# First feed-forward product by seven products instead of eight (Strassen), in a one-core encoder layer in float32

## Chip, cores and metric

One core of one Trainium2 chip runs the kernel. The metric is the device time of one execution in microseconds (us). Five engines work side by side: TensorE (PE; its weight loads are listed as PEld), VectorE (DVE), ScalarE (ACT), GpSimd (POOL) and SyncE (SP), whose queue starts the DMAs. They meet only at semaphores; each engine takes its own instructions in the order in which the program lists them.

## The reference, cut to what matters

The program is one layer of an encoder for 1024 prompt tokens and 128 sample tokens: an input projection, three mixers (forgetting attention, pooling, attention to a memory), a gated merge, an output projection, and a feed-forward part. The change is about the last two lines, and a little about the column block `f` of the input projection.

```
z = rmsnorm(x, g_attn) @ w_in          # ... f: 8 forget logits, logf = log_sigmoid(f + b_f)
h = x + m @ w_out                      # m: the gated sum of the three mixers
a = relu(rmsnorm(h, g_mlp) @ w_up)     # w_up 1024 x 4096
y = h + (a * a) @ w_down               # w_down 4096 x 1024
```

All is float32. The 1152 tokens of both groups go through the weights together.

## The kernel before

**Products in two parts.** A float32 operand is split into a high part that TensorE takes in its `fp32r` form (a rounding copy by ACT, `activation(..., Copy)`) and a low part (DVE: operand minus high part). A product is three matmuls, `COMBOS`: high by high, high by low, low by high. A weight tile is 128 rows by 128 columns for each of the 8 slices of the model width (`KT` = 8), a block is one output tile by a third of the tokens (`TB` = 384 columns), so a block over the model width is 8 x 3 = 24 matmuls of 384 columns. Blocks go to three PSUM banks in turn (`bank(b)`, banks 5 to 7); `emptied(eng, b)` waits until the block has been read out, `finished(eng, b)` until its matmuls are done.

**Order.** There is no scheduler: `plan` is a list of steps (`add(kind, i, j, ...)`), and each engine's program walks through it and issues its own share of every step (`for s in plan[FIRST:]`), with extra work hung beside a step by `put(...)`. For the steps `out`, `up`, `down` and `last`:

- `out` n (8 of them, 3 blocks of 24 matmuls): one tile of `m @ w_out`. DVE adds the block to `H`, ACT and DVE write the next product's operand `A` (times `g_mlp`, high and low) and the squares for the norm.
- `up` (8 rounds of 4 tiles, 3 blocks each): one row tile of `w_up`. DVE reads the block (`ff_r`: relu times 1/rms, L2041), squares it (`ff_a`, L2044) and subtracts the high part that ACT made of it (`ff_hi` L1497, `ff_lo` L2047).
- `down` (7 rounds of 8 tiles, 3 blocks of 12 matmuls): the four tiles of `up` times `w_down`, added to `H` by DVE (L2052). `last` is the eighth round, with its weights (`w_last`) loaded as a whole, and the output norm beside it.

Weights of all these steps come by one DMA a tile, are split by `split_hi` (ACT, L444) and `split_lo` (DVE, L451), and are kept twice (`W[c % 2]`), so a tile is made ready while the one before it is used.

**The start.** `early` makes the first blocks beside the normalisation of x. The forget logits are 8 columns, but the tile loaded for them is 128 columns wide, and takes the same 24 matmuls a block as any other.

**GpSimd** makes constants at the start and sixteen small copies for the sample tokens (L800), and nothing from 802 us on.

## Time and profile before

| | |
|---|---|
| median of 3 runs | 2033.2 us (2032.01 to 2034.89) |
| the profiled execution | 2032.71 us; its span 2031.0 us |
| PE busy | 1969.2 us (97%), 11755 matmuls; granted clock 0.994 |
| DVE busy | 992.2 us (49%) |
| ACT busy | 690.5 us (34%) |
| POOL busy | 10.7 us (1%) |
| DMA | 164.7 MB, mean 81 GB/s |
| PE in 1212.2 to 1964.3 us (`up` and `down`) | busy all of 752.1 us |

The span runs from the first to the last instruction; the time is 1.7 us longer. A busy share adds up instruction durations, and matmuls overlap: a matmul of 384 columns is listed with about 0.33 us, while one starts every 0.174 us. So PE's pace is read from distances between starts, or from a count over a stretch, not from durations.

### The profile page before, as it was taken

To read this page: it belongs to the slowest core of one execution; us is meant where nothing else is said; L and a number is where in the kernel's file an instruction comes from. 1 tells how busy PE (TensorE), PEld (TensorE's weight loads), DVE (VectorE), ACT (ScalarE), POOL (GpSimd) and SP (SyncE) were. 2 spreads that over 40 slices of the span, in tenths; PEclk is the share of its full clock that TensorE was granted. 3 is DMA by queue.
4 is the path that set the end of the run, shared out by engine and by line. 5 is a ranking of instruction groups with operands and counts; after the bars stand their busy time and mean duration, and the time that the engine had idled before them with its cause. 6 is when DMAs were issued, how large, how long until landed. Compare 5 with 4: busy or idle time off the path is not lost.

```text
span 2031.0 us, 28635 instructions
## 1 busy us (share of the span) xinstructions
PE 1969.2 (97%) x11755; PEld 1936.3 (95%) x11755; DVE 992.2 (49%) x1895; ACT 690.5 (34%) x1299; POOL 10.7 (1%) x45
## 2 busy tenths in 40 slices
PE   7998999999989999999999999999999999999998
PEld 7998899999989989999999999999999999999998
DVE  6674545454446656554433455444343434344434
ACT  6444546364555545443222332111111111111112
POOL 0000000000000000000000000000000000000000
PEclk9999999999999999999999999999999999999999
DMA  6442221212245544254223311020202020202202
GB/s 189 111 111 61 57 84 37 82 56 69 72 155 179 167 149 130 89 165 149 82 79 91 89 54 42 27 58 27 58 27 57 27 57 27 57 27 57 69 26 93
DMA packets 208087, 164.72 MB, mean 81 GB/s; under 512 B 14287, under 2 KB 186319, under 8 KB 207446
## 3 DMA queue, kind: packets, MB, share of 16 engines
q1 hardware_dynamic: 207957, 162.90, 26.4%
q8 instruction: 93, 1.52, 0.3%
q14 instruction: 37, 0.30, 0.0%
HBM read 133.36 MB, written 29.51 MB: 80 GB/s over the span
## 4 chain that ended last, share of the span: by engine, by line
PE 81%; issue 6%; ACT 6%; DVE 5%; DMA 2%; SPq 0%; ACTq 0%; DVEq 0%
PE ps L1150 68%; PE ps L1134 2%; PE ps L986 2%; PE ps L976 1%; PE ps L822 1%; ACT fox_p L1299 1%; PE ps L909 1%; ACT fox_pt_hi L1306 1%; PE ps L943 1%; ACT fox_p L1311 1%; ACT w_hi L444 1%; PE ps L919 1%; DVE fox_pt_lo L1729 1%; DMA foxs_kraw<-in_cache_fox_k_dram 0%; PE ps L1056 0%
## 5 line engine op out<-in xcount | busy, mean ns | idle before, releaser
L1150 PE MATMUL ps<-act_hi,w_hi 128*128 128x384 f32 x1800 | 612.7, 340 | 4.7 <-DVE fox_v L1995 3.5
L1150 PE MATMUL ps<-act_hi,w_lo 128*128 128x384 f32 x1800 | 603.2, 335 | 0.0
L1150 PE MATMUL ps<-act_lo,w_hi 128*128 128x384 f32 x1800 | 602.9, 335 | 0.0
L1150 PEld LDWEIGHTS ps<-act_hi,w_hi 128*128 128x128 f32 x1800 | 338.7, 188 | 6.6 <-issue 5.7
L1150 PEld LDWEIGHTS ps<-act_lo,w_hi 128*128 128x128 f32 x1800 | 338.9, 188 | 0.7
L1150 PEld LDWEIGHTS ps<-act_hi,w_lo 128*128 128x128 f32 x1800 | 338.3, 188 | 0.0
L444 ACT ACTIVATE w_hi<-w_raw 128x1024 fp32r<-128x1024 f32 (+1 forms) x173 | 148.1, 856 | 302.4 <-PE ps L1150 300.8
L451 DVE TENSOR_TENSOR w_lo<-w_raw,w_hi 128x1024 fp32r<-128x1024 f32 (+1 forms) x173 | 168.8, 976 | 133.2 <-ACT w_hi L444 133.2
L1150 PE MATMUL ps<-ff_hi,w_hi 128*128 128x384 f32 x672 | 227.1, 338 | 0.0
L1150 PE MATMUL ps<-ff_lo,w_hi 128*128 128x384 f32 x672 | 227.1, 338 | 0.0
L1150 PE MATMUL ps<-ff_hi,w_lo 128*128 128x384 f32 x672 | 227.1, 338 | 0.0
L2052 DVE TENSOR_TENSOR h<-ps,h 128x384 f32<-128x384 f32 x192 | 106.9, 557 | 222.5 <-PE ps L1150 199.1
L1497 ACT ACTIVATE ff_hi<-ff_r 128x384 fp32r<-128x384 f32 x96 | 50.4, 525 | 325.7 <-DVE ff_r L2041 325.7
L2041 DVE SCALAR_TENSOR_TENSOR ff_r<-ps,rstd 128x384 f32<-128x384 f32 x96 | 53.4, 557 | 185.1 <-PE ps L1150 185.1
L1150 PEld LDWEIGHTS ps<-ff_hi,w_hi 128*128 128x128 f32 x672 | 126.2, 188 | 0.0
L1150 PEld LDWEIGHTS ps<-ff_hi,w_lo 128*128 128x128 f32 x672 | 126.2, 188 | 0.0
L1150 PEld LDWEIGHTS ps<-ff_lo,w_hi 128*128 128x128 f32 x672 | 126.2, 188 | 0.0
L1150 PE MATMUL ps<-branch_hi,w_hi 128*128 128x384 f32 x288 | 102.0, 354 | 0.0
L1150 PE MATMUL ps<-branch_hi,w_lo 128*128 128x384 f32 x288 | 98.2, 341 | 0.0
L1150 PE MATMUL ps<-branch_lo,w_hi 128*128 128x384 f32 x288 | 98.1, 341 | 0.0
L1729 DVE TENSOR_TENSOR fox_pt_lo<-ps,fox_pt_hi 128x128 fp32r<-128x128 f32 (+3 forms) x64 | 48.5, 758 | 86.2 <-ACT fox_pt_hi L1306 85.9
L1573 ACT ACTIVATE gate<-ps 128x384 f32<-128x384 f32 x72 | 35.3, 490 | 103.2 <-PE ps L1150 103.2
(306 smaller groups left out, 2830.3 us busy)
## 6 DMA issues: line engine op xcount, KB each, us to landing
w_raw<-in_w_in_dram SPq DMA_DIRECT2D x45, 512.0 KB, 4.5
w_raw<-in_w_up_dram SPq DMA_DIRECT2D x32, 512.0 KB, 4.1
w_raw<-in_w_down_dram SPq DMA_DIRECT2D x56, 256.0 KB, 2.8
merged<-prod SPq DMA_DIRECT2D x48, 192.0 KB, 1.9
prev<-merged SPq DMA_DIRECT2D x48, 192.0 KB, 4.2
foxs_kraw<-in_cache_fox_k_dram SPq DMA_DIRECT2D x8, 1024.0 KB, 5.2
foxs_vraw<-in_cache_fox_v_dram SPq DMA_DIRECT2D x8, 1024.0 KB, 5.7
out_dram<-fin_y SPq DMA_DIRECT2D x9, 512.0 KB, 2.6
```

The source lines that it names most:

```text
L444: nc.scalar.activation(W[c % 2][0][:, 0:kt, :], w_raw[c % 2][:, 0:kt, :], ACT.Copy).then_inc(w_hi[c % 2], 1)
L451: nc.vector.tensor_tensor(W[c % 2][1][:, 0:kt, :], w_raw[c % 2][:, 0:kt, :], W[c % 2][0][:, 0:kt, :].bitcast(F32), ALU.subtract).then_inc( ...
L822: last = nc.tensor.matmul(bank(s.b)[:, 0:TB], W[k][a][:, t, :], A[z][:, t, cols(s.j)], start=(t == 0 and n == 0), stop=(t == KT - 1 and n ...
L909: last = nc.tensor.matmul(ps[:, 4, lo:2 * P], fv[:, x, 2 * h:2 * h + 2, :], fpt[z][:, x, lo:2 * P], start=(x == 0 and z == 0), stop=(x == ...
L986: last = nc.tensor.matmul(ps[:, 4, :], b["pt"][x][:, t, :], b["v"][y][:, t, :], start=(n == 0 and t == 0), stop=end)
L1134: last = nc.tensor.matmul(bank(s.b)[:, 0:TB], LW[a][:, t, s.j * P:(s.j + 1) * P], AC[(NCH - 1) % 2][z][:, t, cols(s.i)], start=(t == 0 and ...
L1150: last = nc.tensor.matmul(bank(b)[:, 0:width], W[k][a][:, t, :], moving[z][:, t, j * width:(j + 1) * width], start=(t == 0 and n == 0), st ...
L1497: nc.scalar.activation(AC[s.i % 2][0][:, s.j, cols(j)], ff_r[i % 2][:], ACT.Square).then_inc(ff["hi"], 1)
L1573: nc.scalar.activation(gate[:, cols(j)], src, ACT.Tanh, scale=0.5).then_inc(free, 1)
L1729: nc.vector.tensor_tensor(dst[1][:, 0:blocks, cs], turned_tiles()[:, 0:blocks, :], dst[0][:, 0:blocks, cs].bitcast(F32), ALU.subtract).the ...
L2041: nc.vector.scalar_tensor_tensor(out=ff_r[i % 2][:], in0=src, scalar=0.0, in1=rstd[:, cols(j)], op0=ALU.max, op1=ALU.mult).then_inc(free, 1)
L2052: nc.vector.tensor_tensor(h, src, h, ALU.add).then_inc(free, 1)
```

## The change

**Strassen on `up`.** The product of `w_up` with h is taken in pairs of row tiles. With the model width cut into two halves of 4 slices (`HK`), the weights of a pair are a 2 x 2 matrix of blocks; the tokens are cut into two halves (`HALF` = 576), each half into two quarters (`TQ` = 288 columns), so that the h operand of a half is 2 x 2 as well. Seven products (m = 0 to 6) of sums of such blocks take the place of eight: 7 x 4 x 3 = 84 matmuls of 288 columns for a pair of row tiles and a half of the tokens. There are 16 pairs x 2 halves = 32 such groups g, two to each step `up(c)`, and they come as `up(0) up(1) down(0) up(2) down(1)` and so on; `down(c)` takes place for one half of the tokens. Around the seven products stands new work:

- the h operands: 7 sums for each slice (`BS`, `BO`), on ACT, DVE and POOL, once for each half of the tokens;
- the weight operands: for each group five sums of 128x512 on POOL (`weight_sum`), seven rounding copies on ACT (`weight_hi`) and seven subtractions on DVE (`weight_lo`). Each of the seven operands has one buffer (`WO[m]`), so product m of a group must be over before that of the next group is made;
- the results: ACT copies five of the seven products out of PSUM (c3, c4, c1, c5, c2 in that order), POOL makes two combined terms of them by four instructions of 128x288 (`copies_sum`), DVE adds one of the four terms to a product still in PSUM (`result`, first instruction), multiplies by 1/rms (second), and squares and splits (`square_lo`, two more). PSUM banks 0 to 4 take the products in turn; a bank is free for the product five later only once it has been read.

**`out`, `down`, `last`** go by quarters of the tokens: 4 blocks of 288 columns where there were 3 of 384. A `down` step holds two output tiles (weights 128x1024 at once).

**Forget logits.** Only the 8 columns are loaded; their high parts go to columns 0 to 7 and their low parts to columns 32 to 39 of one tile, zeroed by POOL, so two matmuls a slice do (`pairs`) where there were three; DVE adds the two halves of the result.

**Smaller**: several semaphores are merged, DVE makes `g_neg` behind the load of `g_mlp`, the 1/rms is made once for each half of the tokens.

The core of the diff:

```diff
+    HALF, TQ = T // 2, T // 4
+    HK = KT // 2
+    PAIRS_UP = FT
...
+    for c in range(2 * NCH):
+        up(c)
+        if c % NCH:
+            down(c - 1)
+        if c == NCH - 1:
+            down(c)
...
+            def weight_sum(g, m):
...
+                if g:
+                    pool.wait_ge(up_s["over"], 7 * (g - 1) + m + 1)
...
+                nc.gpsimd.tensor_tensor(WS[m][:], up_raw(g, *a), up_raw(g, *b), op).then_inc(uw["sum"], 1)
...
+            def copies_sum(g, n):
+                pool.wait_ge(up_s["copied"], 5 * g + 4 + n)
+                a, out = ((c4, c5), (c3, c2))[n]
+                nc.gpsimd.tensor_tensor(out[:], a[:], out[:], ALU.subtract).then_inc(up_s["e"], 1)
+                pool.wait_ge(up_s["e"], 4 * g + 2 * n + 1)
+                nc.gpsimd.tensor_tensor(out[:], out[:], c1[:], ALU.add).then_inc(up_s["e"], 1)
...
+            def up_product(g, x):
...
+                pe.wait_ge(uw["lo"], 7 * g + x + 1)
+                if 7 * g + x >= 5:
+                    bank_left(pe, *divmod(7 * g + x - 5, 7))
...
+                        last = nc.tensor.matmul(up_bank(g, x), WO[x][a][:, t, :], BO[x][z][:, t, :],
+                                                start=(t == 0 and n == 0), stop=(t == HK - 1 and n == 2))
...
+                    nc.scalar.activation((c3, c4, c1, c5, c2)[x][:], up_bank(g, x), ACT.Copy).then_inc(up_s["copied"], 1)
...
+            def weight_lo(g, m):
+                dve.wait_ge(uw["hi"], 7 * g + m + 1)
...
+                nc.vector.tensor_tensor(WO[m][1][:], src, WO[m][0][:].bitcast(F32), ALU.subtract).then_inc(uw["lo"], 1)
...
+            def result(g, n, other):
...
+                nc.vector.tensor_tensor(out[:], up_bank(g, x), other[:], ALU.add).then_inc(up_s["step"], 1)
...
+                nc.vector.scalar_tensor_tensor(out=out[:], in0=out[:], scalar=0.0,
+                                               in1=rstd[:, quarter(2 * g // PAIRS_UP, RESULT[n][1])], op0=ALU.max,
+                                               op1=ALU.mult).then_inc(up_s["r"], 1)
+
+            def square_lo(i):
+                out = ff_r[i % 3]
+                dve.wait_ge(ff["hi"], i + 1)
+                nc.vector.tensor_tensor(out[:], out[:], out[:], ALU.mult).then_inc(ff["a"], 1)
+                dve.wait_ge(ff["a"], i + 1)
+                nc.vector.tensor_tensor(ff_part(1, i), out[:], ff_part(0, i).bitcast(F32), ALU.subtract).then_inc(ff["lo"], 1)
...
+                pairs = COMBOS if s.kind == "u" else ((0, 0), (0, 1))
```

The second group of an `up` step gets its weight operands 0 to 3 during the first group (`weights_at`), and 4 to 6 at its own first products; the first group of the next step gets all seven during the `down` step between.

What DVE has in its program inside `up` in the kernel before, three blocks and a weight tile (`ff_r`, `ff_a`, `ff1_lo`: the result, its square, the square's low part; `w0_lo`: the weight tile's low part; `ffn_hi` is counted up by ACT, `blk_over` by PE):

```order
L2041 SCALAR_TENSOR_TENSOR ff_r0_205<-ps,rstd_204 128x384 [waits blk_over]
L2044 TENSOR_TENSOR ff_a0_207<-ff_r0_205 128x384 [waits bank_free2]
L2047 TENSOR_TENSOR ff1_lo_203<-ff_a0_207,ff1_hi_202 128x384 [waits ffn_hi,ffn_a]
L2041 SCALAR_TENSOR_TENSOR ff_r1_206<-ps,rstd_204 128x384 [waits blk_over]
L2044 TENSOR_TENSOR ff_a1_208<-ff_r1_206 128x384 [waits bank_free0]
L2047 TENSOR_TENSOR ff1_lo_203<-ff_a1_208,ff1_hi_202 128x384 [waits ffn_hi,ffn_a]
L451 TENSOR_TENSOR w0_lo_57<-w_raw0_54,w0_hi_56 128x1024 [waits w_hi0]
```

Each result needs three instructions, of which the first reads PSUM, and each weight tile adds one more to every nine.

What DVE has in the changed kernel at the passage from the first group of an `up` step to its second (`u_c2`, `u_c5`: the terms that POOL has made, `up_e` counts POOL's steps; `ffm_lo`: low part of the squares; `u_op4_lo` to `u_op6_lo`: low parts of the second group's weight operands, `up_w_hi` is counted by ACT):

```order
L2239 TENSOR_TENSOR ff_r0_253<-ps,u_c2_252 128x288 [waits up_over,up_e]
L2243 SCALAR_TENSOR_TENSOR ff_r0_253<-ff_r0_253,rstd_197 128x288 [waits up_step]
L2239 TENSOR_TENSOR ff_r1_254<-ps,u_c5_251 128x288 [waits up_over]
L2243 SCALAR_TENSOR_TENSOR ff_r1_254<-ff_r1_254,rstd_197 128x288 [waits up_step]
L2250 TENSOR_TENSOR ff_r0_253<-ff_r0_253 128x288 [waits ffn_hi]
L2252 TENSOR_TENSOR ffm_lo_247<-ff_r0_253,ffm_hi_246 128x288 [waits ffn_a]
L2250 TENSOR_TENSOR ff_r1_254<-ff_r1_254 128x288 [waits ffn_hi]
L2252 TENSOR_TENSOR ffm_lo_247<-ff_r1_254,ffm_hi_246 128x288 [waits ffn_a]
L2232 TENSOR_TENSOR u_op4_lo_234<-u_sum4_243,u_op4_hi_233 128x512 [waits up_w_hi]
L2232 TENSOR_TENSOR u_op5_lo_236<-u_sum5_244,u_op5_hi_235 128x512 [waits up_w_hi]
L2232 TENSOR_TENSOR u_op6_lo_238<-u_sum6_245,u_op6_hi_237 128x512 [waits up_w_hi]
L2239 TENSOR_TENSOR ff_r2_255<-ps,u_c3_248 128x288 [waits up_over,up_copied]
```

Results now take four instructions, two of the group's four results stand behind POOL's `up_e`, and the weight operands that PE needs for products 4 to 6 of the second group stand behind all of the first group's results.

What POOL has in the same stretch (`u_sum`: sums of weight blocks, `u_raw1`: the loaded pair; `up_over` is counted by PE for each product, `up_copied` by ACT for each copy); before, POOL had no instruction here at all:

```order
L950 TENSOR_TENSOR u_sum2_241<-u_raw1_224 128x512 [waits up_over,u_in1]
L956 TENSOR_TENSOR u_c5_251<-u_c4_249,u_c5_251 128x288 [waits up_copied]
L958 TENSOR_TENSOR u_c5_251<-u_c5_251,u_c1_250 128x288 [waits up_e]
L950 TENSOR_TENSOR u_sum3_242<-u_raw1_224 128x512 [waits up_over]
L956 TENSOR_TENSOR u_c2_252<-u_c3_248,u_c2_252 128x288 [waits up_copied]
L958 TENSOR_TENSOR u_c2_252<-u_c2_252,u_c1_250 128x288 [waits up_e]
L950 TENSOR_TENSOR u_sum4_243<-u_raw1_224 128x512 [waits up_over]
L950 TENSOR_TENSOR u_sum5_244<-u_raw1_224 128x512 [waits up_over]
L950 TENSOR_TENSOR u_sum6_245<-u_raw1_224 128x512 [waits up_over]
```

The sum for weight operand 3 stands between the two combined terms, and the sums for operands 4 to 6 behind them.

## Rows read from the trace of the kernel before

**Rows 1.** Busy time by stretch: start:end, length, busy us (count) by engine, clock.

```profile
1212.20:1964.30 752.10, 752.10 (x4310) 752.10 (x4309) 337.97 (x548) 119.51 (x189) 0.00 (x0) 1.00 0.15 43
...
1300.00:1500.00 200.00, 200.00 (x1147) 200.00 (x1146) 85.94 (x142) 29.91 (x48) 0.00 (x0) 1.00 0.15 43
```

**Rows 2.** Chain that ended last: start us, length us, what, count of matmuls.

```profile
1212.22 752.15 PE ps L1150 x4308
```

**Rows 3.** Waits over the whole span: us in total, times, longest us.

```profile
ACT ff_hi L1497 <- DVE ff_r L2041: 325.7, 96, 6.9
...
DVE h L2052 <- PE ps L1150: 199.1, 152, 1.6
...
DVE ff_r L2041 <- PE ps L1150: 185.1, 92, 2.4
```

**Rows 4.** Timeline of PE, weights by memory tokens: start us, us, instruction; 22 between.

```profile
103.17 0.28 PE L1150 MATMUL ps<-memn_hi,w_hi 128*128 128x256 f32 x1
...
105.92 0.28 PE L1150 MATMUL ps<-memn_hi,w_lo 128*128 128x256 f32 x1
```

**Rows 5.** Instruction groups of DVE, 1205 to 1400 us: busy us, mean ns.

```profile
L2047 DVE TENSOR_TENSOR ff_lo<-ff_a,ff_hi 128x384 fp32r<-128x384 f32 x33 | 18.4, 558 | 2.3
...
L2052 DVE TENSOR_TENSOR h<-ps,h 128x384 f32<-128x384 f32 x24 | 13.4, 557 | 28.7 <-PE ps L1150 28.7
...
L451 DVE TENSOR_TENSOR w_lo<-w_raw,w_hi 128x1024 fp32r<-128x1024 f32 x11 | 13.5, 1225 | 4.0 <-ACT w_hi L444 4.0
...
L451 DVE TENSOR_TENSOR w_lo<-w_raw,w_hi 128x512 fp32r<-128x512 f32 x9 | 6.2, 690 | 1.0 <-ACT w_hi L444 1.0
...
L1914 DVE RECIPROCAL rstd<-rstd 128x384 f32<-128x384 f32 x3 | 7.4, 2514 | 1.4 <-ACT rstd L1436 1.4
```

**Rows 6.** Instruction groups of ACT in the same stretch.

```profile
L1497 ACT ACTIVATE ff_hi<-ff_r 128x384 fp32r<-128x384 f32 x33 | 17.3, 525 | 109.3 <-DVE ff_r L2041 109.3
...
L444 ACT ACTIVATE w_hi<-w_raw 128x512 fp32r<-128x512 f32 x9 | 5.6, 627 | 33.3 <-PE ps L1150 33.3
```

**Rows 7.** Timeline of DVE in `up`: start us, us, instruction.

```profile
1226.84 0.56 DVE L2041 SCALAR_TENSOR_TENSOR ff_r<-ps,rstd 128x384 f32<-128x384 f32 x1
...
1227.43 0.56 DVE L2044 TENSOR_TENSOR ff_a<-ff_r 128x384 f32<-128x384 f32 x1
...
1228.06 0.56 DVE L2047 TENSOR_TENSOR ff_lo<-ff_a,ff_hi 128x384 fp32r<-128x384 f32 x1
```

**Rows 8.** Instruction groups of POOL, whole span: busy us, mean ns.

```profile
L800 POOL CAST foxs_kt_lo<-ks_lo 128x64 fp32r<-128x64 f32 x8 | 1.9, 234 | 0.0
...
L779 POOL MEMSET ident<- 128x128 f32 x1 | 0.2, 204 | 0.0
...
L778 POOL MEMSET eps_t<- 128x1 f32 x1 | 0.1, 98 | 0.3 <-POOLq L2082 0.3
```

**Rows 9.** Timeline of DVE and POOL near 595 us.

```profile
594.48 1.29 DVE L1798 TENSOR_TENSOR foxs_kt_lo<-ps,foxs_kt_hi 128x512 fp32r<-128x512 f32 x2
...
595.01 0.24 POOL L800 CAST foxs_kt_hi<-ks_hi 128x64 fp32r<-128x64 f32 x1 [591.50 <-DMA o_fox<-fox_o]
```

**Rows 10.** Timeline of DVE and POOL near 632 us.

```profile
631.42 0.67 DVE L1897 TENSOR_TENSOR foxs_vn_lo<-foxs_vnraw,foxs_vn_hi 16x512 fp32r<-16x512 f32 x1
...
631.73 1.62 POOL L800 CAST foxs_kt_hi<-ks_hi 128x64 fp32r<-128x64 f32 x1 [15.05 <-PE ps L976]
...
632.02 1.21 DVE L1904 TENSOR_TENSOR branch_lo<-branch_raw,branch_hi 128x1024 fp32r<-128x1024 f32 x1
...
633.30 0.23 POOL L800 CAST foxs_kt_lo<-ks_lo 128x64 fp32r<-128x64 f32 x1
```

**Rows 11.** Instruction group of PE in the early blocks.

```profile
L822 PE MATMUL ps<-act_lo,w_hi 128*128 128x384 f32 x48 | 16.3, 340 | 0.0
```

**Rows 12.** Chain that ended last, a piece in the early blocks.

```profile
34.38 6.27 PE ps L822 x36
```

More of the change, by code:

```diff
@@ L1591, in _ @@
                         leave(s, x // per)
+                    if s.kind == "out" and s.i % 2 and x == 3:
+                        token_parts(0, s.i // 2)
+                    for m in token_steps(s, x):
+                        token_hi(0, s.i // 2, m)
+                        if s.i == KT - 1:
+                            weight_hi(0, m)
             for t in range(6, NT):
```

546 lines of the change are left out of this document (400 added, 146 removed).

## The prediction, on record before the changed kernel ran

> **What bounds the kernel now.** I read the busy shares by stretch first, then the chain of waits, then the list of waits, then single instructions. From 1212 to 1964 us, `up` and `down`, PE is busy all the time at full clock (1.00, the 2.4 GHz level), DVE for 338 us of 752 and ACT for 120 [rows 1]; the chain that ended last is in this stretch one unbroken piece of PE [rows 2]. The long waits are those of DVE and ACT for PE: DVE waits 199 us for `down` blocks and 185 us for `up` blocks [rows 3]. So PE's matmuls are worth their full time here, and DVE has about half its time to spare: 86 us busy in 200 [rows 1], on average. The change spends that spare time unevenly, and this is what decides.
>
> **The matmuls.** `up` and `down` hold 96 x 24 + 168 x 12 = 4320 matmuls of 384 columns (a few are missing in the record) in 752.15 us [rows 2]: 174.1 ns each. Matmuls of 256 columns with a new weight tile each start 23 steps apart in 2.75 us [rows 4]: 119.6 ns. The line through both is 0.426 ns a column, so 288 columns cost 133.2 ns; weight loads do not hold back even 256 columns. Then:
> - `up`: 2304 x 174.1 ns = 401.1 us becomes 2688 x 133.2 ns = 358.0 us: -43.1
> - `out`: 576 becomes 768 matmuls, 100.3 to 102.3 us: +2.0
> - `down` and `last`: 2304 become 3072 (15 x 16 blocks of 12, and 16 more), 401.1 to 409.2 us: +8.1
>
> An eighth of the columns goes, but the fixed part of every matmul comes a third more often in the rest. Sum -33 us; with 1 ns of error in the 133.2, 6.5 us either way.
>
> **Forget logits.** 24 of the early matmuls go. They are dense there: 36 in 6.27 us, 174 ns each [rows 12], of three kinds with 48 each [rows 11]. That is 4.2 us if they all lie on the path, 0 if the normalisation of x ends last. I take -3. The additions (DVE once, ACT three short ones) lie beside PE.
>
> **What stands around the seven products.** Sizes first. DVE takes 558 ns for 384 columns and 690 for 512 [rows 5], so 1.03 ns a column and 459 ns for 288. Where one waits for the one before, starts are 0.59 and 0.63 us apart for 0.56 us of work [rows 7]: I take 0.50 us for 288 and 0.65 for a weight operand. ACT: 525 and 627 ns for 384 and 512 columns [rows 6], 0.45 for 288, 0.63 for a weight operand. A group needs 16 DVE instructions for its four results and 7 weight subtractions: 8.0 + 4.6 = 12.6 us, against 84 x 133.2 ns = 11.2 us of PE. A step of two groups has 7 of the 14 subtractions moved to the `down` before it, and so 20.5 us of DVE in 22.4 of PE; but no result can be taken before the first group's fourth product is over (6.6 us), and DVE is then full until the end of the step. ACT has about 16 us in 22.4; for it only the order matters.
>
> POOL is the unknown: no two-input instruction stands in the trace. A memset of 1 and of 128 elements takes 98 and 204 ns, 0.83 ns an element; a cast of 64 takes 234 ns, over 98 ns that is 2.1 an element [rows 8]. So the sum of 128x512 costs between 0.52 and 1.2 us, that of 128x288 between 0.34 and 0.7. A cast reads and writes as a sum does, so it is nearer, and I take its end: 1.2 and 0.7. That is 10 x 1.2 + 8 x 0.7 = 17.6 us of POOL in a step and its `down`, of 48.0 us of PE.
>
> The second unknown is whether POOL and DVE can work at once. Beside DVE instructions with one input in SBUF (the other in PSUM), POOL's cast takes its 0.24 us [rows 9]. But behind a DVE instruction with both inputs in SBUF it is listed with 1.62 us, and ends at 633.35, only when that one and the next like it, begun at 632.02 for 1.21 us, are over; the cast behind it takes 0.23 again [rows 10]. So POOL stands still through such an instruction of DVE, and gets no turn between two that follow closely. Of DVE's new instructions all but the first of each result have both inputs in SBUF. Whether POOL holds up DVE in turn the trace cannot show: its casts were too short.
> The Trainium skill ("SBUF — State Buffer", Who interferes with whom) says it does: whichever starts first has the shared port for its whole instruction, and the rule covers a DVE instruction with two SBUF inputs against a GpSimd one that reads. Rows 10 agree with one half of it; no row bears on the other. By it the forecast below holds at its middle or above.
> The skill's "GPSIMD Engine Reference" (Elementwise — side-by-side cycle accounting) gives 2.6 cycles an element for a two-input instruction; an estimate from that page is 1.1 us for 512, near the upper end, and no row has one.
>
> **The timetable of a step** (us from its first product; PE 1.6 a product, results 0.2 after its last matmul). Operand 2 of the second group: product over 5.0, POOL's sum until 6.3, ACT 7.0, DVE 7.7. ACT stands behind that sum, so it copies product 3 only by 7.45. POOL's two steps on it are broken by DVE's second instruction of the first result: 9.55. Then the sum for operand 3: 10.75, ACT's copy of it 11.4; the copy of product 4, over at 8.2, stands behind it in ACT: 11.85. DVE splits operand 3 until 12.1. From here DVE has, before it may split operand 4, three results (3.0), their two finished squares and the third (4.0 with the last one's), and 0.65: 7.5 to 8 us; and POOL has two steps and the three sums for operands 4 to 6, 1.4 + 3.6 = 5.0, all due now. Side by side they would end at 20; one after the other, but for the 1.5 us in which DVE reads PSUM, at 24. PE wants operand 4 at 17.6, and product 3's bank (the third result) at 16.0. So PE stands for 6.4 us in the second group: 2.4 by the late start of this stretch (12.1) and 4 by the port inside it. Behind the step DVE runs late by 16 more instructions and the weight tile (1.2 us), and POOL has the next five sums (6.0) beside it; `down` has three banks of slack, 4.8 us. In POOL's favour every time, that costs another 5 us; in DVE's, nothing more, and of the 6.4 some 4 remain. A step thus loses 4 to 11 us; I take 7, the 6.4 and a little of the tail. 16 steps: +112 us (64 to 176). What is queued behind each new wait: in ACT, behind the copy of operand 3, the copy of product 4, and for that POOL's second term and with it DVE's third result; in DVE, behind the third and fourth result, the squares and operands 4 to 6, for which PE waits; in SP only the next pair of `w_up`, due a group later.
>
> **Around it.** The first operands: 10.7 us of DVE (4 `H` and norm instructions, 3 + 7 token parts, 7 weight operands) in the last 6.4 us of `out`: about 4 us late. The second half's token operands put 10 DVE instructions (4.6 us) in one piece before a `down` block, four times, about 1 us of stall each; its 1/rms, 2 reciprocals of 1.9 us (2514 ns for 384 columns [rows 5]), lie in a `down`. Together +8 (0 to 15).
>
> **Sum.** -33 - 3 + 112 + 8 = +84 us. The profiled execution took 2032.7 us, its span 2031.0 and 1.7 around it; the median of the runs is 0.5 above it. 2033.2 + 84 = 2117 us.
>
> **Rivals.**
> - *The cover holds*: POOL at the lower end, no port shared, DVE's queue just fits. Then only -33 - 3 is left: 1997 us. For it: on average DVE has 20.5 of 22.4 us. Against: 32 DVE instructions and 5 operand splits follow the 7.05 us point, 19.3 us, and end at 26.3, then the weight tile and the first `down` result at 28.3, which PE wants at 27.2.
> - *DVE's queue alone*: POOL fast or out of the way, but that 1.1 us is paid at 14 of the passages into `down`: +15, and +5 around. 2033.2 - 36 + 20 = 2017 us. This is the side on which the change pays. It decides if POOL's instructions take under 0.6 us and the port is free: the sum for operand 3 is then there at 8.35 instead of 10.75.
> - *POOL slow, port free*: operand 4 is ready at 18.9 instead of 17.6 and the first `down` result another 1.3 late: 2.6 us a step, +42, and +8: 2047 us. For it: nothing shows DVE held up. Against: POOL itself was held up, which delays its sums all the same.
> - *POOL always first*: 11 us a step, +176, and +8: 2181 us. At such stops PE's clock may fall too; before, it stood at 1.00 in this stretch.
>
> **Chances.** The forecast 0.50 (2070 to 2150), POOL always first 0.12, POOL slow with a free port 0.11, DVE's queue alone 0.19, cover holds 0.08. What this kernel's measurement can tell from no change is about 0.2%, 4 us. Faster holds the last two, 0.27; within 0.2% is the low edge of the third, 0.03; slower is the rest, 0.70. The range 2012 to 2185 leaves out the cover, a little of DVE's queue alone, and half of POOL always first; the forecast's own is 2070 to 2150.
>
> **What would show it.** Right: matmuls of 288 columns 133 ns apart; POOL's 128x512 sums listed at 1.2 us or more, with far longer ones where DVE works; DVE's 128x288 instructions with two SBUF inputs longer than 0.46 us; PE idle several us before the fourth and fifth product of each second group, released by DVE's `ff_r` or `u_op_lo`, and before the fourth block of a `down`. PE's share of busy time falls from 97% towards 90%. Wrong: PE busy throughout `up`, or the idle time elsewhere, above all at the first products of a first group; or matmuls of 288 columns slower than 140 ns, which would cost 45 us without any wait.

## The result, and the profile after

The changed kernel took **2214.9 us** (median of 4 runs, 2214.1 to 2219.8) where the kernel before took 2034.1 us: 1.089 times as long, 95% interval 1.088 to 1.090, or +181 us. The forecast was +84 us. The direction and the mechanism held. The loss of a step was put at half of what it is, and a part of it, PE's half clock, stood in no term.

The page of the changed kernel first: busy us with share and count by engine, then PE and its granted clock in 40 slices of 55 us.

```profile
span 2211.7 us, 32943 instructions
...
PE 1999.5 (90%) x13077; PEld 1950.0 (88%) x13077; DVE 1366.7 (62%) x2453; ACT 890.3 (40%) x1755; POOL 379.2 (17%) x350
...
PE   7999999999899999999998788888889788888898
...
PEclk9999999999999999999999898988999999889899
```

PE's share is 90%, as the prediction's last part had it, and its eights and sevens lie, but for three slices, in slices 22 to 38, in `up` and `down`. The clock is not 1.00 there any more, as it was in [rows 1].

**Where the time is.** The first product of `up` starts at 1205.9 us (1211.8 before), the first of `last` at 2169.8 (1964.2 before). So the head got 6 us shorter and the stretch from `up` to `last` went from 752 to 964 us. It holds 2688 + 2880 = 5568 matmuls of 288 columns. A piece of the chain of waits gives their pace, 36 in 4.80 us, 133.3 ns; all of them are worth 742 us. The stretch loses 222 us, 13.9 for each of 16 steps. The rest of the +181 is `last`, which now covers only half of the tokens: from its first product to the end it takes 41.9 us in place of 66.8, so that -6, +212 and -25 add up.

The waits of PE from 1200 to 2150 us (us in total, times, longest us), where before it had none in `up` and `down` [rows 2]:

```profile
PE ps L1338 <- DVE h L2400: 73.5, 18, 7.7
PE ps L1323 <- DVE ff_r L2239: 38.2, 14, 2.8
PE ps L1323 <- DVE u_op_lo L2232: 35.7, 27, 5.9
```

That is 147 us in which PE stands: L1338 is `down`, L1323 the products, and all three are released by DVE. In [rows 3] it was DVE that waited for PE. One period from 1411.65 to 1473.66, from one step's stop in `down` to the next's, shows all of it. The chain of waits (start us, us, what):

```profile
1411.65 23.20 PE ps L1338 x156
1434.84 4.80 PE ps L1323 x36
...
1439.78 1.30 POOL u_sum L950
...
1442.11 1.03 POOL u_c L956
1443.21 0.90 POOL u_c L958
1444.11 1.26 POOL u_sum L950
...
1445.40 0.64 ACT u_op_hi L1689
...
1447.15 0.58 DVE ff_r L2243
1447.74 1.00 DVE ff_r L2250
...
1448.76 1.44 DVE ffm_lo L2252
1450.20 1.47 DVE ff_r L2250
```

From the first group's fourth product on, the chain leaves PE and goes through POOL's sums and DVE's squares, as the timetable of the prediction said. The three stops of PE in this period (timeline; idle before it and its releaser in brackets):

```profile
1453.61 0.37 PE L1323 MATMUL ps<-b_op_hi,u_op_hi 128*128 128x288 f32 x1 [2.78 <-DVE ff_r L2239]
...
1457.19 0.61 PE L1323 MATMUL ps<-b_op_hi,u_op_hi 128*128 128x288 f32 x1 [0.91 <-DVE u_op_lo L2232]
...
1473.66 0.61 PE L1338 MATMUL ps<-ffm_hi,w_hi 128*128 128x288 f32 x1 [4.91 <-DVE h L2400]
```

They stand before the second group's fourth product, before its fifth, and before the fourth block of `down`.

**The port, both ways.** Groups of POOL and of DVE, 1200 to 2150 us (busy us, mean ns of one):

```profile
L950 POOL TENSOR_TENSOR u_sum<-u_raw 128x512 f32<-128x512 f32 x160 | 232.4, 1476 | 436.2 <-PE ps L1323 436.2
L956 POOL TENSOR_TENSOR u_c<-u_c,u_c 128x288 f32<-128x288 f32 x64 | 64.0, 999 | 141.2 <-ACT u_c L1705 141.2
```
```profile
L2250 DVE TENSOR_TENSOR ff_r<-ff_r 128x288 f32<-128x288 f32 x128 | 118.5, 926 | 0.0
L2252 DVE TENSOR_TENSOR ffm_lo<-ff_r,ffm_hi 128x288 fp32r<-128x288 f32 x128 | 114.7, 896 | 4.4
...
L2243 DVE SCALAR_TENSOR_TENSOR ff_r<-ff_r,rstd 128x288 f32<-128x288 f32 x128 | 87.1, 680 | 4.6
...
L2239 DVE TENSOR_TENSOR ff_r<-ps,u_c 128x288 f32<-128x288 f32 x128 | 57.5, 449 | 12.3 <-ACT u_c L1705 11.8
```

DVE's instruction with one input in PSUM (L2239) takes 449 ns; the three of the same size with both in SBUF take 680 to 926. Single instructions of L2250 take 444 ns when POOL is idle and up to 1547. POOL's sum takes 1262 ns at least. The timeline near 1401 us (DVE, then POOL) shows the turns:

```profile
1401.37 1.54 DVE L2250 TENSOR_TENSOR ff_r<-ff_r 128x288 f32<-128x288 f32 x1
1402.95 1.44 DVE L2252 TENSOR_TENSOR ffm_lo<-ff_r,ffm_hi 128x288 fp32r<-128x288 f32 x1
1404.31 0.45 DVE L2239 TENSOR_TENSOR ff_r<-ps,u_c 128x288 f32<-128x288 f32 x1
1404.79 1.07 DVE L2243 SCALAR_TENSOR_TENSOR ff_r<-ff_r,rstd 128x288 f32<-128x288 f32 x1
1405.78 0.45 DVE L2239 TENSOR_TENSOR ff_r<-ps,u_c 128x288 f32<-128x288 f32 x1
1406.26 1.04 DVE L2243 SCALAR_TENSOR_TENSOR ff_r<-ff_r,rstd 128x288 f32<-128x288 f32 x1
1407.22 1.52 DVE L2250 TENSOR_TENSOR ff_r<-ff_r 128x288 f32<-128x288 f32 x1
1408.77 0.46 DVE L2252 TENSOR_TENSOR ffm_lo<-ff_r,ffm_hi 128x288 fp32r<-128x288 f32 x1
```
```profile
1401.10 7.33 POOL L950 TENSOR_TENSOR u_sum<-u_raw 128x512 f32<-128x512 f32 x5
```

While POOL's five sums run (until 1408.4), each of DVE's instructions with two SBUF inputs first waits for the POOL instruction under way: five of them take 6.6 us in place of 2.3. With the first instruction after the last sum the time is 0.46 again, and the two that read PSUM never wait. Neither engine gets ahead: they take turns, one instruction each. The Trainium skill ("SBUF — State Buffer", Who interferes with whom) says that a DVE instruction with two SBUF inputs contends with a GpSimd instruction that reads SBUF; [rows 10] had shown one half of it, these rows show the other. So the engines do not meet at semaphores only, as the section on the chip had it: these two meet here as well, with no semaphore between them.

**PE's clock.** Busy us of each engine with counts, then the granted clock, in stretches right behind two stops:

```profile
1411.60:1416.60 5.00, 4.95 (x20) 4.96 (x21) 2.90 (x6) 1.61 (x3) 0.00 (x0) 0.50 0.32 105
...
1457.20:1460.50 3.30, 3.30 (x14) 3.30 (x15) 2.18 (x4) 0.87 (x4) 1.91 (x2) 0.50 0.22 44
```

After the stop of 5.6 us, PE runs 5 us at a granted clock of 0.50, the 1.2 GHz level, with matmuls 240 ns apart (single ones start at 1412.05 and 1412.29), and is back at 133 ns by 1417. In the whole stretch of `up` and `down` 548 matmuls follow one another by about 240 ns; that is 58 us more than at 133 ns, and most of the 75 us that the 147 of waits leave open. It is in no term of the prediction's sum. How much of it costs time is the question of experiment 6.

### The profile page after: what moved, and what is told of

Read it like the earlier page. It is cut to its first block, busy times and chain, and to the rows that moved or that the text cites. A ratio compares the mean times of both kernels' runs of the same rounds, so it can differ in the third digit from the quotient of the medians.

```text
span 2211.7 us, 32943 instructions
## 1 busy us (share of the span) xinstructions
PE 1999.5 (90%) x13077; PEld 1950.0 (88%) x13077; DVE 1366.7 (62%) x2453; ACT 890.3 (40%) x1755; POOL 379.2 (17%) x350
## 4 chain that ended last, share of the span: by engine, by line
PE 57%; DVE 22%; issue 9%; ACT 7%; POOL 3%; DMA 2%; SPq 0%; ACTq 0%; DVEq 0%; POOLq 0%
PE ps L1368 27%; PE ps L1338 15%; PE ps L1323 5%; DVE ff_r L2250 5%; DVE ff_r L2243 3%; DVE ffm_lo L2252 3%; DVE ff_r L2239 2%; PE ps L1162 2%; DVE u_op_lo L2232 2%; POOL u_sum L950 2%; DVE w_lo L506 1%; PE ps L1152 1%; ACT fox_pt_hi L1521 1%; ACT fox_p L1514 1%; PE ps L1085 1%
## 5 line engine op out<-in xcount | busy, mean ns | idle before, releaser
L1338 PE MATMUL ps<-ffm_hi,w_hi 128*128 128x288 f32 x960 | 297.7, 310 | 73.5 <-DVE h L2400 73.5
L1368 PE MATMUL ps<-act_hi,w_hi 128*128 128x384 f32 x1032 | 356.0, 345 | 6.0 <-DVE fox_v L2357 3.5
L1323 PE MATMUL ps<-b_op_hi,u_op_hi 128*128 128x288 f32 x896 | 284.6, 318 | 73.9 <-DVE ff_r L2239 38.2
L1368 PE MATMUL ps<-act_hi,w_lo 128*128 128x384 f32 x1032 | 346.8, 336 | 0.0
L1368 PE MATMUL ps<-act_lo,w_hi 128*128 128x384 f32 x1032 | 346.2, 335 | 0.0
L950 POOL TENSOR_TENSOR u_sum<-u_raw 128x512 f32<-128x512 f32 x160 | 232.4, 1476 | 436.2 <-PE ps L1323 436.2
L1338 PE MATMUL ps<-ffm_lo,w_hi 128*128 128x288 f32 x960 | 294.8, 307 | 0.0
L1338 PE MATMUL ps<-ffm_hi,w_lo 128*128 128x288 f32 x960 | 294.3, 307 | 0.0
L1323 PE MATMUL ps<-b_op_lo,u_op_hi 128*128 128x288 f32 x896 | 279.7, 312 | 0.0
L1323 PE MATMUL ps<-b_op_hi,u_op_lo 128*128 128x288 f32 x896 | 279.4, 312 | 0.0
L1338 PEld LDWEIGHTS ps<-ffm_hi,w_hi 128*128 128x128 f32 x960 | 192.2, 200 | 78.0 <-DVE h L2400 78.0
L1323 PEld LDWEIGHTS ps<-b_op_hi,u_op_hi 128*128 128x128 f32 x896 | 182.2, 203 | 85.0 <-DVE u_op_lo L2232 43.8
L1338 PEld LDWEIGHTS ps<-ffm_lo,w_hi 128*128 128x128 f32 x960 | 192.2, 200 | 0.0
L1338 PEld LDWEIGHTS ps<-ffm_hi,w_lo 128*128 128x128 f32 x960 | 192.0, 200 | 0.0
L1323 PEld LDWEIGHTS ps<-b_op_hi,u_op_lo 128*128 128x128 f32 x896 | 183.6, 205 | 0.0
L1323 PEld LDWEIGHTS ps<-b_op_lo,u_op_hi 128*128 128x128 f32 x896 | 182.8, 204 | 0.1
```

The costliest lines, as they stand in the source:

```text
L950: nc.gpsimd.tensor_tensor(WS[m][:], up_raw(g, *a), up_raw(g, *b), op).then_inc(uw["sum"], 1)
L1323: last = nc.tensor.matmul(up_bank(g, x), WO[x][a][:, t, :], BO[x][z][:, t, :], start=(t == 0 and n == 0), stop=(t == HK - 1 and n == 2))
L1338: last = nc.tensor.matmul(bank(s.b + j)[:, 0:TQ], wide(W[s.c % 2][a], CH, 2 * P)[:, t, n * P:(n + 1) * P], FF[z][:, CH * (s.i % 2) + t, qu ...
L1368: last = nc.tensor.matmul(bank(b)[:, 0:width], W[k][a][:, t, :], moving[z][:, t, j * width:(j + 1) * width], start=(t == 0 and n == 0), st ...
```

## The experiments

In the table, "PE waits" is PE's waiting for DVE from 1200 us on. a_memset, a_small, a_mw, a_mc and a_copy leave out the sums that are named; the others compute all of it. The kernels whose names begin with b run the steps in the order of experiment 4, the others in that of the changed kernel.

| kernel | us | ratio to before, 95% | PE waits, us | clock |
|---|---|---|---|---|
| changed kernel | 2214.9 | 1.0878 to 1.0904 | 148 | 0.955 |
| a_memset: all sums as memsets | 2016.9 | 0.9894 to 0.9935 | 12 | 0.993 |
| a_small: sums of an eighth or less | 2013.0 | 0.9875 to 0.9915 | 11 | 0.992 |
| b_inter: half a `down` behind each group | 2258.9 | 1.1088 to 1.1121 | 190 | 0.944 |
| b_inter_act: and the square on ACT | 2210.1 | 1.0847 to 1.0884 | 141 | 0.950 |
| b_gate: b_inter, weight sums only after the results | 2173.4 | 1.0639 to 1.0717 | 120 | 0.965 |
| b_gate_act: and the square on ACT | 2155.5 | 1.0569 to 1.0606 | 114 | 0.974 |
| b_dve: b_inter, square on ACT, sums on DVE | 2117.5 | 1.0386 to 1.0421 | 74 | 0.975 |
| a_mw: weight sums as memsets | 2058.0 | 1.0098 to 1.0134 | 50 | 0.989 |
| a_mc: result sums as memsets | 2172.5 | 1.0656 to 1.0690 | 122 | 0.966 |
| a_copy: a_mc, weight sums as copies | 2047.9 | 1.0032 to 1.0072 | 35 | 0.989 |
| a_dve: all sums on DVE | 2101.8 | 1.0306 to 1.0347 | 72 | 0.980 |
| a_act_dve: and the square on ACT | 2056.2 | 1.0091 to 1.0124 | 40 | 0.989 |
| a_last: and `down` read out first | 2046.4 | 1.0039 to 1.0080 | 28 | 0.988 |
| a_last_cs: a_last, result sums on POOL | 2051.5 | 1.0058 to 1.0089 | 33 | 0.984 |
| a_fill: extra matmuls in the stops | 2201.3 | 1.0792 to 1.0841 | 84 | 0.976 |
| a_fill2: the same, placed right | 2187.0 | 1.0738 to 1.0792 | 61 | 0.989 |

**1. The length of POOL's chain, or its reading?** In a_memset each sum is replaced by two memsets, with the same waits. In a_small the sums cover 64 of 512 and 16 of 288 columns. Neither computes the operands.

```diff
# a_memset
-nc.gpsimd.tensor_tensor(WS[m][:], up_raw(g, *a), up_raw(g, *b), op).then_inc(uw["sum"], 1)
+then_next(nc.gpsimd.memset(WS[m][:], 0.5))
+nc.gpsimd.memset(WS[m][:], 0.5).then_inc(uw["sum"], 1)
# a_small
+nc.gpsimd.tensor_tensor(WS[m][:, :, 0:8], up_raw(g, *a)[:, :, 0:8], up_raw(g, *b)[:, :, 0:8], op)...
```

> The changed kernel with each of POOL's sums in the up steps replaced by two memsets of the same tile one after the other (the sums are not computed): by the memset rows of before 0.52 + 0.23 + 0.52 = 1.3 us for 128x512 and 0.9 us for 128x288, as long as the sums take undisturbed in the changed kernel (1.26 and 0.81 us), with the same waits, but POOL reads nothing. Theory (a POOL instruction that reads SBUF and a DVE instruction with two SBUF inputs exclude each other, both ways): DVE's 128x288 instructions fall from 0.68 to 0.93 us back to 0.46, and a step from 62.0 us to about 51 (the chain behind the slow sums stays): 2030 to 2055 us. Rival 1 (the chain behind slow sums does it all, no port): stays at 2190 to 2215 us. Rival 2 (any POOL instruction holds up DVE, writes too): also 2190 to 2215 us, but with DVE's instructions still long.

> The changed kernel with POOL's sums cut to 64 of 512 and 16 of 288 columns (the rest is not computed; ACT and DVE take the weight operands 2 to 6 from the loaded weights instead, so that they do the same amount of work). Theory: POOL is out of the way, only DVE's own queue of 20.5 us in 22.4 is left: 1 to 2 us lost a step, 2010 to 2030 us. Rival (DVE's queue by itself is too long, POOL only adds to it): still over 2100 us.

Measured: 2016.9 and 2013.0 us, both about 1% faster than the kernel before (0.9894 to 0.9935 and 0.9875 to 0.9915 of its time). Groups of a_memset, POOL then DVE:

```profile
L950 POOL MEMSET u_sum<- 128x512 f32 x160 | 84.2, 526 | 384.8 <-PE ps L1326 384.8
```
```profile
L2255 DVE TENSOR_TENSOR ffm_lo<-ff_r,ffm_hi 128x288 fp32r<-128x288 f32 x128 | 58.7, 458 | 4.4
L2253 DVE TENSOR_TENSOR ff_r<-ff_r 128x288 f32<-128x288 f32 x128 | 57.8, 452 | 0.0
```

POOL is busy 1.05 us for each weight operand and DVE's instructions are back at 452 and 458 ns. So a POOL chain of about this length costs 4 us at most (the two kernels differ by that), and nearly all of the 198 us hang on POOL's reading. A pair of memsets is 0.2 us shorter than an undisturbed sum; that this is not the cause is shown by a_copy below, where POOL's instructions are shorter still and cost 31 us. The expectation for a_memset had 13 to 38 us left for the chain; that was a miss, on the small side. a_small came within its range. The Trainium skill ("SBUF — State Buffer", Who interferes with whom) says that a GpSimd instruction that only writes does not contend; these rows agree.

**2. Which sums?** a_mw replaces only the weight sums (L950) by memsets, a_mc only the sums of results (L956, L958), by the same edit.

> Of POOL's work only the five weight sums of a group (128x512) are replaced by two memsets each, of about the same time and with the same waits; the partial sums of results (128x288) stay real. The sums that are replaced are not computed. With both kinds replaced the kernel took 2016.9 us, with both real 2214.9. Theory (a loss has to use up DVE's slack before it costs anything, so the two losses are not additive): the eight short sums of a step, 0.8 us each, hold DVE up by at most 6.4 us in 45, and the slack of DVE takes most of that: 2025 to 2060 us. Rival (each microsecond of shared port costs its share, 6.4 of 19 us of POOL's reading in a step): a third of the 198 us, 2083 us. Second rival (the short sums stand on the path of the results, so they carry the loss): 2120 us or more.

> The other half: the partial sums of results (128x288) on POOL are replaced by two memsets each, and are not computed; the weight sums (128x512) stay real. Theory (the five weight sums in a row behind each group carry the loss, both in the group and in the tail that runs into the down blocks): 2110 to 2170 us, and DVE's first down readout of a step still late by about 5 us. Rival by share of the reading time: two thirds of 198 us, 2149 us, together with 2083 us of the other kernel. Second rival (the short sums carry it): below 2080 us.

Measured: 2058.0 us, just inside its range, and 2172.5 us, 2.5 above its own. Over a_memset the sums of results alone cost 41 us and the weight sums alone 156; together they make 197, and both at once cost 198. The cost is additive, against the theory that a slack has to be used up first. Nor does it go by time alone: the short sums have a third of the reading and a fifth of the cost. It goes by the time that DVE's instructions take longer. From 1200 us to the end DVE is busy for 581 us in a_memset, 618 in a_mw, 703 in a_mc and 737 in the changed kernel: 37, 122 and 156 us more, for a cost of 41, 156 and 198. These, too, add up. In a_mw DVE's squares take 599 ns, in the changed kernel 926:

```profile
L2251 DVE TENSOR_TENSOR ff_r<-ff_r 128x288 f32<-128x288 f32 x128 | 76.7, 599 | 0.0
```

**3. The second input, or reading at all?** a_copy is a_mc with a copy of one operand in place of the weight sum.

```diff
-nc.gpsimd.tensor_tensor(WS[m][:], up_raw(g, *a), up_raw(g, *b), op).then_inc(uw["sum"], 1)
+nc.gpsimd.tensor_copy(WS[m][:], up_raw(g, *a)).then_inc(uw["sum"], 1)
```

> The partial sums of results are memsets again, and are not computed; the five weight sums of a group are replaced by a copy of one 128x512 operand on POOL, one input instead of two, so the operands are not the sums. With real two-input sums in their place the kernel took 2172.5 us, with memsets for both 2016.9. Theory (any POOL instruction that reads SBUF holds the port against DVE's instructions with two SBUF inputs): the loss follows the length of the copy; at 0.5 to 1.2 us each 2080 to 2175 us, and DVE's 128x288 instructions with two SBUF inputs at a mean above 600 ns. Rival (POOL needs the port only for its second input): 2012 to 2030 us, and DVE's at 450 to 480 ns.

```profile
L950 POOL COPY u_sum<-u_raw 128x512 f32<-128x512 f32 x160 | 121.5, 790 | 423.2 <-PE ps L1325 423.2
```
```profile
L2252 DVE TENSOR_TENSOR ff_r<-ff_r 128x288 f32<-128x288 f32 x128 | 77.8, 608 | 0.0
L2254 DVE TENSOR_TENSOR ffm_lo<-ff_r,ffm_hi 128x288 fp32r<-128x288 f32 x128 | 72.9, 570 | 4.4
```

A copy with one input holds DVE up too: 608 and 570 ns in place of 452 and 458. That part of the theory holds. The price does not: 2047.9 us, 31 over a_memset where the range began at 63. A copy takes 610 ns at least, half of the 1262 of a sum, and costs a fifth. Here as well the price follows DVE's extra time: DVE is busy for 619 us from 1200 us on, 38 more than in a_memset and about as much as in a_mw, which costs 41. The copies stand in the same place as the sums (five of them from 1415.1 to 1419.2 us, beside DVE's instructions with two SBUF inputs from 1414.0 to 1420.8), but a delayed instruction of DVE there takes up to 0.87 us, not 1.5, and fewer are delayed (of the 384 of 128x288 with two SBUF inputs, 95 take over 0.52 us, in a_mc 131).

**4. Another order.** The changed kernel runs two groups and then a whole `down`. b_inter puts half a `down` (two of the four column pairs) behind every group, so that each group's DVE work finds a `down` beside it. b_inter_act has ACT square the float32 values; b_gate has POOL start its weight sums only when DVE is through with the group's results; b_gate_act has both, and b_dve has the square on ACT and all sums on DVE.

```diff
# b_inter
-for c in range(2 * NCH):
-    up(c)
-    if c % NCH:
-        down(c - 1)
+up(0, 1, 2)
+for c in range(2 * NCH - 1):
+    down(c, 0, 1)
...
+        up(2 * c + 3)
+        down(c, 2, 3)
...
+            up(2 * c + 4)
# b_gate
+pool.wait_ge(ff["lo"], 4 * (g + 1))
 for m in range(2, 7):
     weight_sum(g + 1, m)
# b_inter_act
+nc.scalar.activation(ff_r[i % 3][:], ff_r[i % 3][:], ACT.Square).then_inc(ff["a"], 1)
-nc.vector.tensor_tensor(out[:], out[:], out[:], ALU.mult).then_inc(ff["a"], 1)
```

> The changed kernel whole, in another order of the steps: half a down step after every single group of seven products instead of a whole one after two groups (groups 0 to 2 and 16 to 18 and 30, 31 still follow each other). No work is added or left out. In 24 us of PE there are then 18 us of DVE and 9 us of POOL, of which 5 can lie beside each other. Theory: what PE lost was that port and DVE were overfull only during the pairs; spread out they fit nearly: 1 to 3 us lost in each of 30 half steps, 2010 to 2070 us. Rival (each group's own chain, from product 3 over ACT and POOL back to the bank, is too long in itself): it stays in every group, 2150 us or more.

Measured 2258.9 us, a clear miss, and worse than the changed kernel. Two stops of PE, one group apart:

```profile
1501.62 0.61 PE L1355 MATMUL ps<-ffm_hi,w_hi 128*128 128x288 f32 x1 [5.99 <-DVE h L2417]
...
1534.53 0.61 PE L1355 MATMUL ps<-ffm_hi,w_hi 128*128 128x288 f32 x1 [5.99 <-DVE h L2417]
```

The five weight sums still come behind every group, and so beside DVE's row of squares; the stop of 5 to 6 us that the changed kernel has once in a step comes after each group, nearly twice as often (32 stops at `down` in place of 18).

> As b_inter, and the float32 square of each result is made by ACT instead of DVE (4 of a group's 12 DVE instructions of 128x288 with two SBUF inputs go, ACT gets 1.8 us more in a group). Theory: 2 us of DVE and port less in 24: the loss goes below 1 us a half step, 1995 to 2025 us, faster than the kernel before. Rival: ACT, now with about 12 us in 24 and in the chain of the copies, becomes the late one; no better than b_inter.

> As b_inter, but POOL's five weight sums for the next group wait until DVE has finished the last square of the present one, so that they lie beside the down blocks, where DVE's results have one input in PSUM. Nothing is left out. In b_inter the first down block behind a group was read out late by 6 us, DVE's squares being listed with 0.9 to 1.5 us beside POOL's sums. Theory: this delay goes to about 1 us, what is left is POOL's four steps on the copies: 2030 to 2080 us. Rival (the weight operands now come late, through POOL, ACT and DVE in turn): PE idles before the first products of a group instead, 2150 us or more.

> As b_gate, with the float32 square made by ACT. Theory: 2 us of DVE less behind every group: 2005 to 2045 us. Rival: as for b_gate, 2150 us or more.

> Half a down step behind every group, the float32 square made by ACT, and all of POOL's work in the up steps made by DVE: DVE has 21.4 us in 24 us of PE, and behind product 3 of a group a queue of 8 us and the weight tile before the first down block: about 1 us late each time, 30 times. Theory (no port conflict left, only DVE's queue): 2010 to 2040 us. Rival (DVE's queue is the bound whatever POOL does): over 2080 us.

Measured: 2210.1, 2173.4, 2155.5 (1.0569 to 1.0606) and 2117.5 us (1.0386 to 1.0421). All four miss: b_inter_act ends 185 us above its range and hardly faster than the changed kernel, b_gate, b_gate_act and b_dve 93, 110 and 77 us above theirs. The gate takes 86 us off b_inter, so the overlap of weight sums and squares is worth about that much there (the two runs of b_gate are 12 us apart). The rivals of b_gate and b_gate_act named 2150 us or more, but for late weight operands; these make PE wait for 21 and 23 us, and `down` for 91 and 90. What the order alone costs is seen with a_act_dve of experiment 5, which has the sums and the square on the same engines as b_dve and takes 2056.2 us: 61 us less. The waits of b_dve tell why (1200 to 2150 us):

```profile
DVE ff_r L2256 <- ACT u_c L1694: 163.5, 48, 6.5
...
PE ps L1325 <- DVE h L2417: 66.1, 42, 3.8
```

In a single group no result can be taken before the fourth product is over and copied. DVE idles there up to 6.5 us, has all its work in the second half, and comes 3.8 us late to the `down` behind it. With two groups in a row that idle time of the second is filled by the first group's results. The other order makes a trouble of its own, which the expectations had not seen.

**5. The sums on DVE.** POOL's sums are 10 x 0.68 and 8 x 0.46 us of DVE in a step, 10.5 us. a_dve moves them all, a_act_dve gives the square to ACT besides, a_last also reads out the first `down` block ahead of the pending splits.

```diff
# a_dve
-nc.gpsimd.tensor_tensor(WS[m][:], up_raw(g, *a), up_raw(g, *b), op).then_inc(uw["sum"], 1)
+nc.vector.tensor_tensor(WS[m][:], up_raw(g, *a), up_raw(g, *b), op).then_inc(uw["sum"], 1)
# a_last
+lead = s.kind == "down" and s.j == 0 and x == 0
+if lead:
+    leave(s, 0)
+    ... square_lo(4 * g + 2); square_lo(4 * g + 3)
 if x == 0 and s.c >= 2:
     split_lo(dve, s.c + 1)
```

> The changed kernel in its own order of steps, with the five weight sums and the four instructions on the copies of every group made by DVE instead of POOL (0.65 us and 0.50 us each there, against 1.26 and 0.85 us undisturbed on POOL). All is computed. Theory (the port makes POOL and DVE take turns): one engine alone does the turns in less time, since its instructions are shorter. DVE gets 7 us more in the 22.4 us of a pair: about 8 us lost a step instead of the 14 of the changed kernel, 2110 to 2135 us. Rival (POOL does help, the port costs only part of each instruction): DVE alone is worse than 2215 us.

> The changed kernel's order of blocks, POOL's sums of both kinds done by DVE, and the float32 square of the feed-forward values by ACT instead of DVE. With the sums on DVE alone the kernel took 2101.8 us. The square takes 8 instructions of some 0.46 us off DVE in a step, 3.7 us, and adds 8 of 0.44 to ACT. Theory (DVE's queue is what is late there): 16 times up to 3.7 us less, 2045 to 2085 us. Rival (ACT's queue becomes late, since its copy of a product stands behind the square): 2095 us or more.

> As the kernel before it (sums on DVE, square by ACT), and DVE takes the first down block of a step out of PSUM ahead of the pending splits: the low parts of the group's last two results and of the step's weight tile come behind it. Theory (PE's stop before the fourth down block of a step is DVE coming late to the first one): 1 to 3 us less a step than the kernel without this edit, that is 16 to 48 us less: 2010 to 2050 us. Rival (the stop only moves behind, since the low parts are needed by the next down blocks): the same within 8 us as without the edit.

Measured: 2101.8 us, 8 below its range; 2056.2; 2046.4, within the range but only 10 less than without the edit, between the theory's 16 and the rival's 8. So the busier engine does POOL's 18 instructions of a step as well, and the kernel (a_dve) gets 113 us faster than the changed one, though still 3% slower than the one before. PE's waits in a_last, 1200 to 2160 us:

```profile
PE ps L1308 <- DVE h L2399: 15.2, 17, 3.2
PE ps L1293 <- DVE u_op_lo L2232: 12.0, 9, 2.4
PE ps L1293 <- issue: 5.9, 1, 5.9
```

A step there has a period of 49.2 us (stops at 1327.70 and 1376.86) with one stop of 0.7. What still keeps a_last 12 us above the kernel before are the groups that stand in a row at the start of each half, without a `down` between them: from 1205 to 1283 us PE stands for 14 us. a_last_cs gives the sums of results back to POOL:

> The kernel with the square on ACT and the down readout ahead of the splits, with the partial sums of results (128x288) back on POOL and only the weight sums on DVE. On POOL these partial sums cost 41 us beside the squares on DVE; on DVE they are 4 instructions of 0.46 us a group, 59 us of DVE in all. Theory (ports cost only while DVE works with two SBUF inputs, and the squares that collided have gone to ACT): 2020 to 2045 us, against 2046 with the partial sums on DVE. Rival (POOL's two dependent steps and the port make the third and fourth result late): 2055 us or more.

Measured 2051.5 us, between the two. With DVE's other work out of the way POOL's short sums still take 1005 and 1012 ns and hold DVE's weight splits up (790 ns in place of 685). No kernel with all of the computation beat the one before.

**6. The clock.** a_fill gives PE matmuls of 288 columns that nobody reads, into a free bank, where it would stand. The first try had those of the `up` part behind the stop in place of in it; a_fill2 mends that.

```diff
# a_fill: 17 for x == 4; a_fill2: 18 for x == 3 and 8 for x == 4
+if g & 1 and g > 2 and x in {3: 18, 4: 8}:
+    fill(bank(b)[:, 0:TQ], h, {3: 18, 4: 8}[x])
# both, ahead of the fourth down block of a step
+for k in range(32):
+    nc.tensor.matmul(up_bank(g, 2), ..., start=True, stop=True)
```

> The changed kernel with all its sums on POOL. Ahead of its two longest waits in a step PE is given extra matmuls of 288 columns whose result nobody reads, into a bank that is free: 17 ahead of the fifth product of a second group (2.3 us in a stop of 2.8) and 32 ahead of the fourth block of a down (4.3 us in a stop of 4.9 to 5.6). The ends of the stops are set by DVE and do not move. Theory (after each stop some 5 us of matmuls run at half clock, 240 instead of 133 ns apart, 2.2 us lost each time, about 68 us in all; with PE kept busy the clock does not fall): 2145 to 2180 us, and the granted clock of the whole run back from 0.955 to 0.98 or more. Rival (the stops themselves are all of the loss): 2205 us or more. Second rival (PE's extra reading slows DVE or POOL): above 2220 us.

> As the kernel with the extra matmuls (2201.3 us), but those of the up part stand where the stop is. There they stood ahead of the fifth product of a second group, behind the stop of 2.8 us, and added their own 2.3 us; here 18 stand ahead of the fourth product and 8 ahead of the fifth. A step took 61.3 us in the changed kernel and 59.2 with the misplaced ones. Theory (the half clock behind the stops costs 2.2 us in the down and 1.7 in the last two products of the up part, the rest is hidden because DVE's end does not move): 57.0 to 57.8 us a step and 2150 to 2175 us. Rival (the up part's slow matmuls are hidden altogether behind DVE): what is left is the 2.3 us taken away again, at most 1 us a step less, 2185 us or more.

Measured 2201.3 and 2187.0 us, both under the changed kernel but above what was expected, by 21 and 12 us; the period of a_fill2 was to be 57.0 to 57.8. Its time is the one that its rival named (2185 or more: the slow matmuls of the `up` part cost nothing). One period of each, in the changed kernel and in a_fill2 (length; busy us of PE, its loads, DVE, ACT, POOL; clock):

```profile
1411.65:1473.66 62.01, 53.42 (x361) 52.64 (x361) 42.74 (x67) 18.45 (x36) 21.68 (x18) 0.89 0.21 69
```
```profile
1350.40:1409.26 58.86, 56.30 (x418) 55.64 (x418) 43.06 (x67) 18.53 (x36) 22.02 (x18) 1.00 0.23 72
```

The clock is back at 1.00, and the period goes from 61.3 us (mean of four, 1351.02 to 1596.03) to 58.9. So of the step's 13.3 us over the 48.0 of the matmuls, 2.4 are the half clock and 10.9 are DVE and POOL. The slow matmuls hide in part, since what PE waits for next is not ready earlier. In a_fill2 the extra matmuls and what PE still waits give the three stops at full clock (18, 8 and 32 matmuls of 133 ns, and the idle time in brackets):

```profile
1390.16 0.37 PE L1331 MATMUL ps<-b_op_hi,u_op_hi 128*128 128x288 f32 x1 [0.43 <-DVE ff_r L2254]
1393.75 0.40 PE L1331 MATMUL ps<-b_op_hi,u_op_hi 128*128 128x288 f32 x1 [0.71 <-DVE u_op_lo L2247]
1409.26 0.40 PE L1353 MATMUL ps<-ffm_hi,w_hi 128*128 128x288 f32 x1 [1.42 <-DVE h L2415]
```

2.40 + 0.43 = 2.8 before the fourth product, 1.07 + 0.71 = 1.8 before the fifth, 4.26 + 1.42 = 5.7 in `down`: 10.3 of the 10.9 us.

## Why the prediction came out as it did

- **The matmul pace.** Right. 133.2 ns was forecast, 36 in 4.80 us are 133.3. With the sums out of the way (a_small) the kernel is 20 us under the one before, and the -36 of matmuls and forget logits less its 15 us of remaining waits of PE make -21.
- **Forget logits and `out`.** The first matmul on the memory tokens starts at 50.2 us in place of 54.8, and the head's gain stays between 3.2 and 5.9 us until the start of `out`, where it is 4.5: -3 forecast. At the start of `up` it is 5.9, so that `out` with its norm got 1.4 us shorter where +2 was forecast, for which no run gives the reason. The first operands' 4 us were not late for the first product; they came as the 5.9 us stop behind it.
- **Sizes on DVE and ACT.** 0.50 us was taken for an undisturbed 128x288 and the rows have 0.45 to 0.47; 0.65 for a weight operand, and a_memset has 0.685. ACT's copy took 406 ns (0.45) and its weight operand 624 (0.63).
- **POOL's sizes.** 1.2 and 0.7 us were the upper ends of the bounds, and both are a little low: 1.26 and 0.81 us at least. The estimate of 1.1 us that stood beside them is lower still; the measurement decides.
- **The port.** Right, and now shown both ways. *POOL slow, port free* (2047) falls with a_memset: a slow POOL without the port costs at most 4 us. *DVE's queue alone* (2017) had the conditions that a_small makes, with POOL's sums short and hardly any reading; that took 2013. In the changed kernel the free port is the condition that fails. That a_memset comes within 0.1 us of 2017 is luck, as its POOL instructions are not short. *The cover holds* (1997) falls with a_small, 2013 with hardly any POOL work at all.
- **A step.** This is the step that failed: "A step thus loses 4 to 11 us; I take 7, the 6.4 and a little of the tail. 16 steps: +112 us". The chip lost 13.9 for each of the 16. Three parts, from a_fill2 and the changed kernel:
  - inside the second group 4.6 us, where 6.4 were forecast. The timetable held: counted from 1434.84, the sum for operand 3 ends at 10.5 (10.75 forecast), and operand 4 is ready at 22.3 (24);
  - behind the step 5.7, where 0.6 were. The working had the price: "In POOL's favour every time, that costs another 5 us". It was put with a rival of 0.12. In fact no favour is needed. DVE's instructions and POOL's sums take turns, and with POOL's next instruction always waiting each turn costs DVE most of a sum. Near 1401 us all five sums of the tail are met by one of DVE's instructions each, which together take 4.3 us longer. The 4.8 us of slack of `down` were to cover them. But a_memset, where PE still waits at that place in 19 stops, 5.9 us in the one at 1564 us and 0.2 in each of the others, shows that DVE's own work behind the step just fills that slack;
  - the half clock behind the stops, 2.4 us a step. It stood as an aside under the last rival and in no sum. By a_fill2 it is 28 us of the 181; its extra matmuls do not cover the stops at the start of each half. These, too, make the mean over all 16 steps 13.9 where the period shown has 13.3.
- **The sum.** 16 x (13.9 - 7) = +110 against the forecast. Off that go the +8 "around it", which lie inside the 222 us of the stretch, and 5 us by which the head is better than the -1 of forget logits and `out`: +97, which is what the forecast is off by.
- **The range.** Its upper end, 2185, left out half of *POOL always first* (11 us a step). With the clock kept up the time is 2187, 2 us above that end; the rest of the miss is the half clock.

That DVE just fits without POOL is also the likely reason why the costs of long and short sums add up to within 1 us, though no run varied it. Open is whether a kernel with POOL's weight sums placed beside DVE's reads of PSUM alone could win; that was not tried.

## What to carry to other kernels

Work given to an idle POOL is not free when it reads SBUF: count for each such instruction the DVE instructions with two SBUF inputs beside it, and let each pay for most of one POOL instruction (0.86 us of 1.26 here). If the sum is more than DVE itself would need, give the work to DVE; here that was 113 us. And when an added wait makes PE stand for some us, put the matmuls behind it into the sum at the clock they will get.
